# The last stage of a transformer-like block: 144 tokens by gathered rows instead of 128, 368 by matmul instead of 384

## The reference, cut to what matters

```python
def peer_ffn(h, w_query, sub_keys, u_tab, v_tab):      # h: 512 x 1024; u_tab, v_tab: 16384 x 1024
    q = (h @ w_query).reshape(..., PEER_HEADS, 2, PEER_HALF)
    scores = einsum("blhcd,hckd->blhck", q, sub_keys)   # 8 heads x 2 halves x 128 keys
    s_top, i_top = top_k(scores, 16)
    cand_s = s_top[..., 0, :, None] + s_top[..., 1, None, :]
    cand_i = i_top[..., 0, :, None] * 128 + i_top[..., 1, None, :]
    best_s, pos = top_k(cand_s, 16)
    expert_idx, gates = take(cand_i, pos), softmax(best_s)
    # for each token: 128 pairs of an expert and a gate
    act = gelu(einsum("td,thkd->thk", h, u_tab[expert_idx]))
    return einsum("thk,thkd->td", gates * act, v_tab[expert_idx])
```

## Time and profile before

| | |
|---|---|
| median of 3 runs | 3023.87 us (3023.0 to 3025.26) |
| the profiled execution | 3024.32 us, span of the core 3022.3 us |
| granted TensorE clock, mean | 0.993 |
| busy: PE, PEld, DVE, ACT, POOL | 2950.5, 2427.7, 2000.1, 1077.4, 911.6 us |
| moved by DMA | 564.99 MB, mean 187 GB/s |
| stage `vo`: from the first to the last of its matmuls | 2476.4 to 3018.7 us |

### The profile page before, as it was taken

How to read it: one execution, slowest core, us unless ns; L and a number is a source line. 1 busy time by engine, 2 the same in 40 slices (tenths; PEclk the granted TensorE clock), 3 DMA queues, 4 the chain that set the end, 5 groups by cost and what they waited for, 6 DMA issues and landing times.

```text
span 3022.3 us, 36556 instructions
## 1 busy us (share of the span) xinstructions
PE 2950.5 (98%) x13699; PEld 2427.7 (80%) x13699; DVE 2000.1 (66%) x3378; ACT 1077.4 (36%) x1652; POOL 911.6 (30%) x598
## 2 busy tenths in 40 slices
PE   8999999999999989999998999999999999999999
PEld 7877787887877865676767887888888889999999
DVE  6678635447788889954684288978422237888887
ACT  4266232223322332222453333339522233333332
POOL 0000000002403200000000049777887417656651
PEclk9999999999999999999999999999999999999999
DMA  6157436554354456533216535669966757999995
GB/s 219 48 179 237 135 102 213 191 198 158 127 175 169 133 188 203 165 117 106 92 42 202 188 117 145 137 140 177 192 140 144 241 177 260 352 366 375 341 371 216
DMA packets 331089, 564.99 MB, mean 187 GB/s; under 512 B 128665, under 2 KB 185113, under 8 KB 330529
## 3 DMA queue, kind: packets, MB, share of 16 engines
q1 hardware_dynamic: 202016, 476.96, 46.2%
q0 software_dynamic: 59392, 67.34, 9.0%
q10 hardware_dynamic: 69504, 18.35, 3.0%
HBM read 489.51 MB, written 140.12 MB: 208 GB/s over the span
## 4 chain that ended last, share of the span: by engine, by line
PE 86%; DVE 7%; POOL 2%; ACT 2%; issue 2%; DMA 1%; SPq 0%; ACTq 0%; DVEq 0%; POOLq 0%
PE psum L684 86%; POOL wl L2351 1%; POOL gates_scratch L2371 1%; DVE wl L1542 1%; ACT wh L1122 1%; DVE trig L1637 0%; DVE yb L1754 0%; DVE psum L1918 0%; DMA xc<-xc 0%; DVE lb L1745 0%; DVE trig L1640 0%; DVE trigw L1641 0%; DVE trig L1642 0%; DVE trig L1639 0%; DVE trigw L1638 0%
## 5 line engine op out<-in xcount | busy, mean ns | idle before, releaser
L1542 DVE TENSOR_TENSOR wl<-ring,wh 128x1024 fp32r<-128x1024 f32 (+2 forms) x424 | 500.5, 1183 | 769.8 <-ACT wh L1122 768.3
L684 PE MATMUL psum<-h_hi,wh 128*128 128x512 f32 x2144 | 856.1, 399 | 34.1 <-DVE h_lo L1686 13.2
L684 PE MATMUL psum<-h_hi,wl 128*128 128x512 f32 x2144 | 849.6, 396 | 0.0
L684 PE MATMUL psum<-h_lo,wh 128*128 128x512 f32 x2144 | 849.4, 396 | 0.0
L1122 ACT ACTIVATE wh<-ring 128x1024 fp32r<-128x1024 f32 (+2 forms) x492 | 504.7, 1028 | 582.2 <-PE psum L684 560.7
L684 PEld LDWEIGHTS psum<-h_hi,wh 128*128 128x128 f32 x2144 | 406.0, 189 | 139.0 <-issue 41.0
L2351 POOL TENSOR_TENSOR wl<-ring,wh 128x1024 fp32r<-128x1024 f32 x68 | 176.3, 2595 | 1102.8 <-ACT wh L1122 1102.8
L684 PEld LDWEIGHTS psum<-h_hi,wl 128*128 128x128 f32 x2144 | 405.7, 189 | 95.3
L684 PEld LDWEIGHTS psum<-h_lo,wh 128*128 128x128 f32 x2144 | 406.1, 189 | 90.7 <-issue 1.7
L2371 POOL DMA_INDIRECT gates_scratch<-picks x256 | 419.9, 1640 | 103.9 <-issue 85.5
L684 PE MATMUL psum<-ews_lo,wh 128*128 128x384 f32 x1024 | 348.2, 340 | 0.0
(11 more groups left out here) (403 smaller groups left out, 3789.0 us busy)
## 6 DMA issues: line engine op xcount, KB each, us to landing
ring<-tables SPq DMA_DIRECT2D x256, 512.0 KB, 4.5
rows_scratch<-tables SPq DMA_DIRECT2D x128, 512.0 KB, 5.1
acts_scratch<-ga SPq DMA_DIRECT2D x128, 256.0 KB, 2.2
abuf<-acts_scratch SPq DMA_DIRECT2D x128, 192.0 KB, 5.9
gbuf<-gates_scratch SPq DMA_DIRECT2D x128, 192.0 KB, 7.2
ring<-w_up SPq DMA_DIRECT2D x44, 512.0 KB, 3.5
ring<-w_modb SPq DMA_DIRECT2D x32, 512.0 KB, 3.5
gates_scratch<-zeros SPq DMA_DIRECT2D x16, 1024.0 KB, 6.7
```

The source lines that it names most:

```text
L684: return nc.tensor.matmul(out, lhsT, rhs, start=first, stop=last, **kw)
L1542: TT(wl, slot(t, 0, size[t]), wh.bitcast(F32), ALU.subtract).then_inc(S("low_by_ve"), 1)
```

## The change

The gathered part takes 16 tokens more: the last 16 of the third block (`SX = 16`). TD becomes 368.

- The 3072 matmuls of `expert_out`, and the operations that make `er`, `ews_hi` and `ews_lo`, are 368 columns wide; `abuf` and `gbuf` take 1472 bytes of a row. The scratch for the gates keeps rows of 384 tokens (TDP), so 1536 bytes apart.
- Spreads go from 32 to 28; the staged groups stay at 32 tokens, and the fourth is parked with 16.
- The 16 tokens x 128 picks are packed as 16 more "picks" of all 128 partitions: partition 16 q + t holds the picks 16 q to 16 q + 15 of token t. DVE works out rows and addresses of the third block (five small instructions ahead of the first spread), and SP packs them by eight small DMAs at j = 62 into `wanted`. GpSimd gathers 144 rows and 144 columns of activations, DVE adds 144 rows; the last 16 go to two more accumulators.
- At the end PE sums the 8 x 16 partitions of these two with a matrix `sel` of 0 and 1 (two matmuls of 16 columns for each bank, into columns 368 to 383) before each transpose.

```diff
@@ -41,11 +41,13 @@
 NB = T // P
 JG = 8
 NV = 6
-TD = T - P
+SX = 16
+NPICK = P + SX
+TD = T - NPICK
 NV_ROWS = 10
 COPY_FROM = 40
 
-ONCE = {"vecs": 16, "bsrow": 32, "x": 48, "cum": 64, "keys": 96}
+ONCE = {"vecs": 16, "bsrow": 32, "x": 48, "cum": 64, "keys": 96, "packed": 96 + 16 * (P // SX)}
 PICK_GROUP = 16
 LAG = 8
 SW = 2 * T + 2 * P
@@ -80,6 +82,7 @@
 SPREAD_FROM = 14
 TURN_AT, SPREAD_AT, SPREADS = 44, 52, 2
 TDS, TG = 2 * P, 32
+TDP = NB * P - P
 SPREAD_OF = [[n for n in range((TD - TDS) // 4) if n // SPREADS == j - SPREAD_AT] for j in range(PK)]
 HEAD_ORDER = [(0, 0), (0, 1), (0, 2), (0, 3), (0, 4), (1, 0), (0, 5), (1, 1), (0, 6), (1, 2), (0, 7), (1, 3), (1, 4),
               (1, 5), (1, 6), (1, 7)]
@@ -310,7 +313,7 @@
             return t[:, :].rearrange("p (c w) -> p c w", w=w)
 
         psum = ctx.enter_context(nc.psum_tensor("psum", [P, 8, T], F32))
-        gates_d = nc.dram_tensor("gates_scratch", (P, PK, TD), F32, kind="Internal").ap()
+        gates_d = nc.dram_tensor("gates_scratch", (P, PK, TDP), F32, kind="Internal").ap()
         states_d = nc.dram_tensor("states_scratch", (NS, P, SW), F32, kind="Internal").ap()
         maps_d = nc.dram_tensor("maps_scratch", (NS, KG, 2 * P), F32, kind="Internal").ap()
         parts_d = nc.dram_tensor("parts_scratch", (KS, 2, P, T), F32, kind="Internal").ap()
@@ -414,12 +417,13 @@
         abuf, gbuf = ar("abuf", B, NV, TD), ar("gbuf", B + NV * TD, NV, TD)
         ews, er = both("ews", B + 2 * NV * TD, NV, TD), ar("er", B + 4 * NV * TD, 2, TD)
 
-        accs, act_s, share_of = ar("accs", B + 10240, 2, D), *(ar(n, B + 12288 + k * P, 1, P)[:, 0, :] for k, n in
-                                                               enumerate(("act_s", "share_of")))
+        accs = [ar(f"accs{k}", at, 1, D)[:, 0, :] for k, at in enumerate((B + 10240, B + 11264, 4096, 5120))]
+        act_s, share_of = (ar(n, B + 12288 + k * NPICK, 1, NPICK)[:, 0, :] for k, n in enumerate(("act_s", "share_of")))
         vrow = [ar(f"vrow{k}", B + at, 1, D)[:, 0, :] for k, at in
                 enumerate([16400 + D * k for k in range(7)] + [13312 + D * k for k in range(3)])]
-        row_of, act_of = (ar(n, B + 26640 + k * P, 1, P, U32)[:, 0, :] for k, n in enumerate(("row_of", "act_of")))
-        gate_s = ar("gate_s", B + 26896, 1, P)[:, 0, :]
+        wanted = ar("wanted", B + 26640, 3, NPICK)
+        row_of, act_of, gate_s = wanted[:, 0, :].bitcast(U32), wanted[:, 1, :].bitcast(U32), wanted[:, 2, :]
+        sel = ar("sel", B + 26640 + 3 * NPICK, 1, SX)[:, 0, :]
 
         silu = ar("silu", B + 26000, KD, 2 * MA)
         a1, a2, gm = t3(sm(2 * KD), 2), sm(KD), sm(KD)
@@ -648,7 +652,7 @@
                     sp.wait_ge(S("ew_raw"), b - NV + 1)
                 sp.wait_ge(S(f"act_parked{b % 4}"), 16 * (b // 4 + 1))
                 sp.dma_start(abuf[:, b % NV, :], acts_d[b][:, 0:TD]).then_inc(S(f"gated{b % NV}"), 16)
-                sp.dma_start(gbuf[:, b % NV, :], gates_d[:, b, :]).then_inc(S(f"gated{b % NV}"), 16)
+                sp.dma_start(gbuf[:, b % NV, :], gates_d[:, b, 0:TD]).then_inc(S(f"gated{b % NV}"), 16)
 
             for e in range(R):
                 expert_in_tile(e)
@@ -659,10 +663,16 @@
                     expert_out_tile(j + R - PK)
                 sp.wait_ge(S("ea_ready"), j + 1)
                 sp.dma_start(acts_d[j], ga4[:, j % 4, :]).then_inc(S(f"act_parked{j % 4}"), 16)
+                if j == SPREAD_AT + 10:
+                    sp.wait_ge(S("picks_ready"), NB + 1)
+                    for q in range(P // SX):
+                        at = slice(q * SX, (q + 1) * SX)
+                        sp.dma_start(wanted[at, :, P:NPICK], t3(picks[:, NB - 2, :], P)[P - SX:P, :, at])\
+                            .then_inc(S("once_loaded"), 16)
                 if j == GATES_AT:
                     for tb in range(2):
                         sp.wait_ge(S(f"scattered{tb}"), 16 * PK)
-                        sp.wait_ge(S(f"gates_parked{tb}"), 16 * ((TD - TDS) // TG // 2))
+                        sp.wait_ge(S(f"gates_parked{tb}"), 16 * 2)
                     for b in range(NV):
                         gated(b)
             for v in range(PK):
@@ -1086,9 +1096,12 @@
                     last = three(psum[:, 4 * half + c, 0:TD], whl(e, 4 * kk + c), ews, b % NV, b == 0, b == PK - 1)
                     if m == PK // 2 - 1 and kk == 1:
                         if half == 0 and c == 0:
-                            pe.wait_ge(S("rows_summed"), PK + 1)
+                            pe.wait_ge(S("rows_summed"), NPICK + 1)
                         dc = 4 * half + c
-                        last = nc.tensor.transpose(psum[:, dc, TD:T], accs[:, 0, dc * P:(dc + 1) * P], ident[:, :])
+                        at = slice(dc * P, (dc + 1) * P)
+                        for q in range(2):
+                            mm(psum[:, dc, TD:TD + SX], accs[2 + q][:, at], sel, q == 0, q == 1)
+                        last = nc.tensor.transpose(psum[:, dc, TD + SX:T], accs[0][:, at], ident[:, :])
                         if c < 3:
                             last.then_inc(S("out_summed"), 1)
                 last.then_inc(PE, 1)
@@ -1486,10 +1499,10 @@
                     A(to[:, P:2 * P], one, ACT.Copy, scale=picksT[:, 2, t:t + 1]).then_inc(S("shares_ready"), 1)
 
             def park_gates(n):
-                g, last = n // (TG // 4), n % (TG // 4) == TG // 4 - 1
-                if last:
+                g, t0 = n // (TG // 4), 4 * (n % (TG // 4))
+                if t0 == TG - 4 or n == (TD - TDS) // 4 - 1:
                     act.wait_ge(S("gates_staged"), n + 1)
-                    act.dma_start(gates_d[:, :, TDS + g * TG:TDS + (g + 1) * TG], parked[g % 2])\
+                    act.dma_start(gates_d[:, :, TDS + g * TG:TDS + g * TG + t0 + 4], parked[g % 2][:, :, 0:t0 + 4])\
                         .then_inc(S(f"gates_parked{g % 2}"), 16)
 
             def high_of_gated(b):
@@ -2199,20 +2212,20 @@
                 ve.wait_ge(S("best_exp"), tb + 1)
                 link(v.tensor_reduce(gsum, t3(bexp, TOPK), AX, ALU.add))
                 link(v.reciprocal(grec, gsum))
-                to = gate_s if tb == NB - 1 else picks[:, tb, 2 * P:3 * P]
+                to = gate_s[:, 0:P] if tb == NB - 1 else picks[:, tb, 2 * P:3 * P]
                 link(TT(t3(to, TOPK), t3(bexp, TOPK), grec.unsqueeze(2).to_broadcast([P, PH, TOPK]), ALU.mult))
                 first, second = picks[:, tb, 0:P], picks[:, tb, P:2 * P]
                 if tb == NB - 2:
                     ve.sem_inc(S("picks_ready"), 1)
                 elif tb < NB - 2:
                     link(STT(fa, first, float(P), second, ALU.mult, ALU.add))
-                    link(TS(fb, fa, float(TD), token[:, tb:tb + 1], ALU.mult, ALU.add))
+                    link(TS(fb, fa, float(TDP), token[:, tb:tb + 1], ALU.mult, ALU.add))
                     v.tensor_copy(first.bitcast(U32), fb).then_inc(S("picks_ready"), 1)
                 else:
                     link(STT(fa, second, float(P), first, ALU.mult, ALU.add))
-                    link(v.tensor_copy(row_of, fa))
+                    link(v.tensor_copy(row_of[:, 0:P], fa))
                     link(TS(fb, fa, float(T), token[:, tb:tb + 1], ALU.mult, ALU.add))
-                    v.tensor_copy(act_of, fb).then_inc(S("picks_ready"), 1)
+                    v.tensor_copy(act_of[:, 0:P], fb).then_inc(S("picks_ready"), 1)
             ve.wait_ge(S("one_col_ready"), 3)
             for tb in range(NB):
                 block_picks(tb, 1 if tb >= 2 else 0)
@@ -2247,6 +2260,12 @@
             lows_to(SPREAD_AT)
             ve.wait_ge(S("gates_zeroed"), 16 * 16)
             ve.wait_ge(S("picksT_ready"), 1)
+            first, second = picks[:, NB - 2, 0:P], picks[:, NB - 2, P:2 * P]
+            link(STT(fa, second, float(P), first, ALU.mult, ALU.add))
+            link(TS(fb, fa, float(T), token[:, NB - 2:NB - 1], ALU.mult, ALU.add))
+            link(v.tensor_copy(first.bitcast(U32), fa))
+            link(v.tensor_reduce(sel, ident[:, :].rearrange("p (q t) -> p t q", t=SX), AX, ALU.add))
+            v.tensor_copy(second.bitcast(U32), fb).then_inc(S("picks_ready"), 1)
             link(v.tensor_copy(picks_hi[:, 0:P], picksT[:, 2, 0:P]))
             link(TT(picksT[:, 2, 0:P], picksT[:, 2, 0:P], picks_hi[:, 0:P].bitcast(F32), ALU.subtract))
             for n in range((TD - TDS) // 4):
@@ -2277,8 +2296,8 @@
                     ve.wait_ge(S(f"acts_picked{n % 2}"), 16 * PICK_GROUP * (n // 2 + 1))
                     link(TT(share_of[:, at], act_s[:, at], gate_s[:, at], ALU.mult))
                 ve.wait_ge(S(f"rows_loaded{k // 2 % (NV_ROWS // 2)}"), 32 * (k // NV_ROWS + 1))
-                acc, by = accs[:, k % 2, :], share_of[:, k:k + 1]
-                if k < 2:
+                acc, by = accs[k % 2 + 2 * (k >= P)], share_of[:, k:k + 1]
+                if k % P < 2:
                     ins = TS(acc, vrow[k % NV_ROWS], by, None, ALU.mult)
                 else:
```

(17 more changed lines are left out.)

## The result

The change made the kernel slightly slower: 3034.13 us median of 7 runs (3027.31 to 3037.19) against 3024.03 us for the kernel before (3021.7 to 3026.72, 7 runs). The ratio on record is 1.0025, 95% interval 1.0015 to 1.0034; the two medians alone would give 1.0033. Forecast were 3004 us and 2999 to 3015.

The account below looks back on a forecast made before the run. The prediction took PE's matmul time to bound the kernel. From the profiled 3024.3 us, -21.6 - 1.9 + 1.9 + 2 = -19.6 gave 3004.7, stated as 3004 us because that execution was 0.4 above the median; range 2999 to 3015.

Parts of the forecast that it names:

- Part 1: Last stage on PE: matmuls of 368 instead of 384 columns each save 7.1 ns, -21.6 us in all.
- Part 2: Spreads, bound by PE: 28 instead of 32 give -1.9 us; the added DVE instructions and SP DMAs cost 0.
- Part 3: Transposes at the end: sixteen added matmuls of 16 columns at 0.12 us each, +1.9 us; bounds 0.5 and 3.2.
- Part 4, GpSimd: Gathers in the last stage: a group of 16 rows takes 48.9 us, DVE uses one in 53.0; it fits.
- Part 4, DMA: Transfers in the last stage: a share of 1.026 is needed, dips can be filled, lateness costs +2 us; bounds 0 and +7.
- The slower rival: Transfers keep their dips from `vo18` to `vo125`, share stays 0.95, the kernel gets slower: 3037 us; chance 0.09.
- Part 4, DVE: Row additions in the last stage: about 0.45 us a tile of free time left on average; cost 0.
- GpSimd becomes the bound: Gathers slow down in fuller queues, a group passes 53 us and DVE waits for rows: about +8, 3011 us; chance 0.06.
- the one for being wrong: Sign in the last stage: PE waits for `wl`, so transfers or GpSimd, whichever DVE waited for, were a bound.

Follow-up runs that it names:

- c1: Changed kernel with GpSimd gathering, from row 16 on, one row and one activation column in turn instead of blocks of 16 columns; 3004.78 us, ratio 0.9934.
- Experiment 5: The run c1: changed kernel with rows and activation columns gathered in turn; 3004.78 us, run once more as c2 with 3006.13 us.
- experiment 4: Changed kernel with each row addition on DVE over 512 instead of 1024 columns, same gathers and bytes; 3002.68 us, ratio 0.9919.
- a3: Changed kernel with 2 KB instead of 4 KB gathered for each row from the eleventh row on, same number of gathers and additions; 3030.78 us, ratio 1.0011.
- c2: The kernel of c1 run once more, unchanged, on the same chip as e2; 3006.13 us, ratio 0.9931.
- a1: Changed kernel with 368 columns but only 128 rows gathered and added, the sum of the 16 packed tokens left out; 3007.01 us, ratio 0.9933.
- e2: c1 with row additions due two tiles earlier and DVE also merging the two packed accumulators; 3000.01 us, ratio 0.9913.

## Why the prediction was wrong, point by point

**Part 1, narrower matmuls: right.** The matmuls of 368 columns take 168.5 ns each (505.4 us for 3000), and the stage of c1 takes 505.4 us where 125 x 4.046 = 505.8 were forecast. That neither the weight loads nor a flatter slope would stand in the way was right too.

**Part 2, spreads: right**, -1.9 us as forecast. That the instructions on DVE and the eight DMAs of SP were hidden is not contradicted: the first spread of the kernels that have them begins between 2039.6 and 2046.2 us, that of the kernel before at 2042.7.

**Part 3, the tail: mis-sized.** Forecast were +1.9 us for the sixteen matmuls, less 0.3 for narrower ones. A bank's turn grew from 1.17 to 1.51 us, so the two cost 0.19 us each, not 0.12: the row had 64 columns but not this place between fp32r matmuls. That makes +2.9 us from the merge to the end in c1 (8.5 to 11.4). The rest of the 4.4 us is clock: banks one and two took 2.2 and 2.4 us with 0.52 granted, after a wait of PE of 2.27 us. The wait before was nearly as long (2.05 us) and the clock stayed at 1.00, so that no row warned of it.

**Part 4, GpSimd: this is the step that failed.** "It fits, with 4 us to spare" set 48.9 us for a group of sixteen rows against the 53.0 us in which DVE uses one. Two things were wrong with it. First, it compared averages where the order decides: in the 26 us of a block no row is issued, DVE takes a row every 3.3 us from a stock of ten, and the first new row could be used 9 us after its issue. 26.3 + 9 us are more than ten rows last (33 us), and DVE waited at 2570.9 us, at the first full block. Second, 48.9 us were lengths from a kernel in which DVE had a gap in every tile. Without the gap, some gathers took 2.93 us: the block from 2598.02 us lasted 31.7 us. The two feed each other: late rows make DVE work without gaps, that makes gathers longer, and these make rows late. Experiment 5 shows the first, 4 the second. What each is worth alone stays open: the stock of fifteen rows, against the first alone, gave back only part (3022 us).
The Trainium skill ("SBUF — State Buffer", section "Who interferes with whom") says that a VectorE instruction with two SBUF inputs contends with a GpSimd instruction that reads SBUF. By that rule a gather, which reads its indices there, can be held up by `er`, `wl`, `ews_lo` and the addition, which all have two SBUF inputs. The trace agrees with it only in part: the gather from 2618.76 us isn't done before the addition is 0.9 us under way, but the one from 2579.78 ends at 2581.12, in the middle of a `wl` (from 2580.68). Which of the instructions holds a gather, and by what, no run here separates.

**Part 4, DMA: right, and over-cautious.** A share of 1.026 was said to be needed and to be within reach; c1 ran at 1.02 and 384 GB/s for 360 us with no wait for gates. The +2 us taken for it were not needed. The slower rival that was given 9% (transfers keep their dips, 3037 us) came close in time and in its sign, a share of 0.96 from 2580 to 2940 us. It was right that GpSimd's pause wouldn't be filled. But it let the bytes set the pace, and they didn't: a3 took a fifth of the rate away (281 for 356 GB/s from 2580 to 2940 us) and stayed at 3031.

**Part 4, DVE: the average was right and of no use.** The free time is there in c1 (74.9 us of waits for ACT, 0.6 us a tile; 0.45 was forecast). Costing a fuller DVE at nothing left out that gathers beside a DVE without gaps can take three times as long.

**The rivals.** The cause was in the list, as "GpSimd becomes the bound", with a chance of 0.06 and 3011 us; there it was to come from fuller queues, while experiment 4 shows that DVE's load matters. Its price was some 8 us in all, since PE's slack was taken to absorb most of each delay; the trace has waits for rows of up to 10.1 us, 18.5 us of PE idle, and 7.3 us more in which PE is busy at a lower clock (513.1 busy where 505.8 were enough). Of the signs listed, the one for being wrong came: PE waits for `wl`.

## What to carry to other kernels

When an edit takes the slack of one engine, ask for each engine that shares work with it whether its durations were measured with that slack; gathers that took 0.95 us beside a DVE with gaps took up to 2.93 beside a full one. Check a supply against its consumer over the longest pause, with the stock and the landing time, not over the average of a cycle; sixteen gathers in one block and the same sixteen in turn with rows differed by some 28 us here. And an edit of the order costs nothing to try: it was worth 0 us before the change and the whole of it after.

## What the runs showed of the hardware that was not expected

- The length of a GpSimd indirect DMA instruction follows DVE's load: median 0.997 us for the activations in the kernel before, 1.281 in the changed one, 0.995 with the additions on DVE halved. Beside rounds of DVE of 3.24 us without a gap either two gathers are done in a round (1.28 and 1.34 us) or one (2.93 us).
- A PE wait of 2.3 us was followed by a granted clock of 0.52 over 3.5 us (changed kernel), 0.57 over 8 us (c2), 0.68 over the 16.1 us of all the transposes (a1) or 1.00 (c1). Runs of c1 and c2 spread from 3001.7 to 3010.1 us, those of e2, which has no such wait, from 2998.1 to 3001.4.
- A matmul of 16 columns in plain fp32 between fp32r matmuls cost 0.19 us with two in a row, and 1.29 - (1.17 - 0.04) = 0.16 us when it stood alone; 0.04 us is what six narrower matmuls give back.
